# Hybrid decoder step: the second recurrence's sample outputs taken from the old states, its state update moved behind the output projection

## The reference, cut to what matters

```
S_t = diag(f_t) S_{t-1} + k_t v_t^T        o_t = S_t^T q_t
```

## Time and profile before

| | |
|---|---|
| median of three runs | 1176.42 us (1174.89 to 1178.26) |
| the profiled execution | 1168.96 us |
| its span, first to last instruction | 1167.1 us |
| TensorE matmuls busy | 1078.2 us (92%), 8206 |
| VectorE, ScalarE, GpSimd busy | 658.5, 395.5, 95.5 us |
| mean granted TensorE clock | 0.944 |

### The profile page before, as it was taken

The page is one execution under the profiler, slowest core; times in us unless marked ns, Lnnn a source line. Parts: engine busy times, 40 slices in busy tenths (PEclk is TensorE's granted clock), DMA queues, the critical chain, the costliest instruction groups (busy, mean ns, idle before and its releaser), DMA issues.

```text
span 1167.1 us, 20544 instructions
## 1 busy us (share of the span) xinstructions
PE 1078.2 (92%) x8206; PEld 911.1 (78%) x8206; DVE 658.5 (56%) x1422; ACT 395.5 (34%) x741; POOL 95.5 (8%) x194
## 2 busy tenths in 40 slices
PE   7998999879997999999999988888999789999997
PEld 5878878757873899999998633545888569999997
DVE  6865471334204588987646465565231447999742
ACT  3523221503134444444411313312213454444430
POOL 0010021210000012221000000000000001222100
PEclk9997889958998899999999988889999899999999
DMA  8330125313445555555443676557444465555540
GB/s 320 140 108 8 39 77 181 108 44 107 145 164 204 190 180 181 182 208 195 172 176 133 240 238 224 172 172 271 175 132 176 149 248 187 181 181 192 208 149 38
DMA packets 41569, 192.40 MB, mean 165 GB/s; under 512 B 4603, under 2 KB 5755, under 8 KB 24579
## 3 DMA queue, kind: packets, MB, share of 16 engines
q1 hardware_dynamic: 37298, 175.76, 43.1%
q0 software_dynamic: 3136, 13.76, 3.2%
q10 hardware_dynamic: 1040, 1.57, 0.4%
HBM read 183.72 MB, written 7.35 MB: 164 GB/s over the span
## 4 chain that ended last, share of the span: by engine, by line
PE 73%; issue 9%; DVE 7%; ACT 3%; DMA 3%; SPq 3%; POOL 1%; DVEq 0%; ACTq 0%; POOLq 0%
PE bank L1193 72%; DVE work L1790 2%; PE bank L1196 1%; SPq L625 1%; ACT work L776 1%; DVE work L1793 1%; SPq L611 1%; DMA ring<-in_cv 1%; DMA ring<-in_gu 1%; ACT work_r L776 1%; DVE smx L1874 0%; DVE ring_r L1790 0%; DMA ring<-in_pool_v 0%; DMA x<-in_x 0%; ACT hr L776 0%
## 5 line engine op out<-in xcount | busy, mean ns | idle before, releaser
L1193 PE MATMUL bank<-h,ring 128*128 128x264 f32 x896 | 207.3, 389 | 0.0
L1193 PE MATMUL bank<-h_r,work_r 128*128 128x264 f32 x704 | 200.6, 285 | 0.2 <-DVE sq_r L1793 0.2
L1193 PE MATMUL bank<-h_r,ring_r 128*128 128x264 f32 x704 | 200.2, 284 | 0.0
L1193 PE MATMUL bank<-sq_r,work_r 128*128 128x264 f32 x704 | 199.8, 284 | 0.0
L1193 PEld LDWEIGHTS bank<-h,ring 128*128 128x128 f32 x896 | 170.6, 191 | 31.3 <-issue 2.3
L776 ACT ACTIVATE work_r<-ring 128x2048 fp32r<-128x2048 f32 (+1 forms) x60 | 125.2, 2087 | 202.8 <-PE bank L1193 191.1
L1790 DVE TENSOR_TENSOR ring_r<-ring,work_r 128x2048 fp32r<-128x2048 f32 (+1 forms) x60 | 150.3, 2506 | 47.0 <-ACT work_r L776 47.0
L1193 PE MATMUL bank<-work 64*64 64x64 f32 (+13 forms) x1424 | 118.9, 279 | 24.0 <-ACT work L776 7.4
L1193 PE MATMUL bank<-work_r 128*128 128x264 f32 x704 | 129.7, 285 | 3.3 <-DVE ring_r L1790 3.1
L1193 PEld LDWEIGHTS bank<-h_r,work_r 128*128 128x128 f32 x704 | 132.3, 188 | 0.6 <-DVE sq_r L1793 0.4
L1193 PEld LDWEIGHTS bank<-sq_r,work_r 128*128 128x128 f32 x704 | 132.5, 188 | 0.1
(11 more groups left out here) (251 smaller groups left out, 1165.1 us busy)
## 6 DMA issues: line engine op xcount, KB each, us to landing
ring<-in_gu SPq DMA_DIRECT2D x44, 1024.0 KB, 4.9
ring<-in_down SPq DMA_DIRECT2D x16, 1408.0 KB, 6.0
ring<-in_pool_k SPq DMA_DIRECT2D x64, 256.0 KB, 3.3
ring<-in_pool_v SPq DMA_DIRECT2D x64, 256.0 KB, 3.2
ring<-in_ev_in_a SPq DMA_DIRECT2D x8, 1024.0 KB, 6.8
ring<-in_ev_in_b SPq DMA_DIRECT2D x8, 1024.0 KB, 4.8
ring<-in_ck SPq DMA_DIRECT2D x8, 1024.0 KB, 4.7
ring<-in_cv SPq DMA_DIRECT2D x8, 1024.0 KB, 5.9
```

Source lines behind the costliest of these rows:

```text
L1193: return nc.tensor.matmul(out, lhsT, rhs, start=start, stop=stop, skip_group_check=True)
```

## The change

The sample outputs of the second recurrence are computed from the old states, right behind the input projection and ahead of the transposes: VectorE forms qfs = q f and qks = q k on the samples' 32 columns, TensorE runs 128 matmuls of one column on shs and one of 32 columns with the block-diagonal ones (the sum k . q on all rows of a head), VectorE multiplies by zi and adds into oT. GpSimd's load of the memory rows and its decay of shs wait for that group. `state_update` goes behind the eight tiles of `ev_out` on TensorE and behind `residual_summed` on VectorE; the store of the new states follows it. The first four tiles of `ev_out` are computed in halves: chunks 0 to 3 between and after the heads' sums, chunks 4 to 7 afterwards. In layer 1 the first halves of tiles 0 and 1 of `od_out` go ahead of the wait for the gated unit. mh and mk change places in work. The diff, cut (left out: semaphore names, ScalarE's lines that lose `so_copy`, asserts):

```diff
@@ -210,6 +210,7 @@
     lin("ev_in_b", 16, 2, 2048, 12, lambda m: order.append(("hn", "gdn", m - 12)))
+    order.append(("sO", "hgrn"))
     for t in range(NCH):
@@ -218,14 +219,13 @@
         order.append(("ho", g))
-    for i in range(HC):
-        order.append(("su", "hgrn", i))
-    order.append(("sO", "hgrn"))
     for c in range(HC):
     lin("ev_out", KC, 2, 2048, 4)
+    for i in range(HC):
+        order.append(("su", "hgrn", i))
     memory(0)
@@ -489,6 +489,8 @@
         d2, e = place(e, HC, L)
+        qfs, e = place(e, HC, NS)
+        qks, e = place(e, HC, NS)
         assert e <= WORK - HC * T, e
@@ -500,8 +502,8 @@
-        mh, e = place(0, KC, NM)
-        mk, e = place(e, MH, NM)
+        mh, _ = place(XX + 2048, KC, NM)
+        mk, e = place(2048, MH, NM)
         mv, e = place(e, MH, NM)
@@ -685,7 +687,8 @@
-            pool.wait_ge(shs_in, 16)
+            full(pool, ("sO", "hgrn"))
+            pool.dma_start(h[:, :, 0:NM], A["memx"]).then_inc(memx_in, 16)
             nc.gpsimd.tensor_tensor(shs, shs, zf[:, :, L:T].unsqueeze(3).broadcast_to([128, HC, NS, HD]),
@@ -695,13 +698,15 @@
             store(A["o_hgrn"], SH[0], hg_stored)
-            pool.wait_ge(sst_ready, 8)
-            store(A["o_shs"], shs, hg_stored)
-                full(pool, ("lin", "ev_in_b", 15) if l == 0 else ("sx", "moba"))
-                pool.dma_start(h[:, :, 0:NM], A["memx"]).then_inc(memx_in, 16)
+                if l == 0:
+                    pool.wait_ge(sst_ready, 8)
+                    store(A["o_shs"], shs, hg_stored)
+                else:
+                    full(pool, ("sx", "moba"))
+                    pool.dma_start(h[:, :, 0:NM], A["memx"]).then_inc(memx_in, 16)
                 pool.wait_ge(hn_done, hn_no[(f"memk{l}", MH - 1)] + 1)
@@ -1000,13 +1005,12 @@
                 o_copy(("ho", (t, p)), p, 0, t)
-            so_copy("hgrn")
+            for g in G4:
+                drained(act, ("ho", g))
             headnorm("hgrn", HC, T, 1.0 / HD, out_rows("hgrn"))
                 act.wait_ge(memx_in, 16 * (l + 1))
-
-                act.wait_ge(hg_stored if l == 0 else kv_stored, 32)
                 for m in range(KC):
@@ -1014,6 +1018,8 @@
             def memory(l):
+                if l:
+                    act.wait_ge(kv_stored, 32)
                 for m in range(MH):
@@ -1049,6 +1055,8 @@
                 samples_out(name, mos, MH)
+                if l == 0:
+                    act.wait_ge(hg_stored, 32)
                 weights_high(l, 0)
@@ -1243,6 +1251,19 @@
                 end(ins)
+
+            def half_product(name, m, k0, src, ready=None):
+
+                b = open_(("lin", name, m)) if k0 == 0 else bank(("lin", name, m))
+                s = slot_of[(name, m)]
+                pe.wait_ge(ring_full[s % SLOTS], slot_value[s])
+                for k in range(k0, k0 + 4):
+                    if ready and m == 0:
+                        ready(k)
+                    o = ((m % 2) * KC + k) * 128
+                    ins = mm(b[:, 0:T], ring[:, s % SLOTS, o:o + 128], src[:, k, 0:T], k == 0, k == KC - 1)
+                if k0:
+                    close(ins, ("lin", name, m))
@@ -1475,6 +1496,15 @@
                     hn("gdn", m - 12, T, bd)
+            pe.wait_ge(hq_ready, 1)
+            pe.wait_ge(shs_in, 16)
+            b = begin(("sO", "hgrn"))
+            for c in range(HC):
+                for s in range(NS):
+                    for p in range(2):
+                        ps = slice(64 * p, 64 * p + 64)
+                        mm(b[ps, c * NS + s:c * NS + s + 1], shs[ps, c, s, :], qfs[ps, c, s:s + 1])
+            end(mm(b[:, 32:64], bd, qks.rearrange("p c s -> p (c s)")))
             pe.wait_ge(hg_dve, 2)
@@ -1521,14 +1551,19 @@
                                     close(ins, ("ho", (t, p)))
-            state_update("hgrn", hws2, 3)
-            state_out("hgrn", shs, zq, 2)
+            pe.wait_ge(mix_ready, 4)
+            half_product("ev_out", 0, 0, mix)
             for c in range(HC):
                 hn("hgrn", c, T, bd)
-            for m in range(KC):
-                if m == 4:
-                    norm(norms.index(("memkv", 0)))
-                lin("ev_out", m, KC, 2, mix, T, lambda k: pe.wait_ge(mix_ready, k + 1))
+                if c % 2:
+                    half_product("ev_out", 1 + c // 2, 0, mix)
+            half_product("ev_out", 3, 0, mix)
+            for m in range(4):
+                half_product("ev_out", m, 4, mix, lambda k: pe.wait_ge(mix_ready, k + 1))
+            norm(norms.index(("memkv", 0)))
+            for m in range(4, KC):
+                lin("ev_out", m, KC, 2, mix, T)
+            state_update("hgrn", hws2, 3)
@@ -1769,10 +1804,14 @@
                 drained(pe, ("O", "moba", j))
+            drained(pe, ("sx", "moba"))
+            for m in range(2):
+                half_product("od_out", m, 0, mix)
             for c in range(HC):
                 drained(pe, ("lin", "glu", 2 * c))
-            drained(pe, ("sx", "moba"))
-            for m in range(KC):
+            for m in range(2):
+                half_product("od_out", m, 4, mix)
+            for m in range(2, KC):
                 if m == 4:
@@ -2153,9 +2192,17 @@
             tt(kx, kx, zk[:, :, 0:L], ALU.mult).then_inc(hg_dve, 1)
+            tt(qfs, zq[:, :, L:T], zf[:, :, L:T], ALU.mult)
+            tt(qks, zq[:, :, L:T], zk[:, :, L:T], ALU.mult).then_inc(hq_ready, 1)
             dve.wait_ge(zg_ready, 4)
                      gated(zg, 0))
+            drained(dve, ("lin", "ev_in_b", 11))
+            full(dve, ("sO", "hgrn"))
+            b = bank(("sO", "hgrn"))
+            ob, pb = [b[:, 32 * i:32 * i + 32].rearrange("p (c s) -> p c s", c=HC) for i in range(2)]
+            step(tt(qks, zi[:, :, L:T], pb, ALU.mult))
+            drain(tt(oT[:, :, L:T], qks, ob, ALU.add), ("sO", "hgrn"))
             dve.wait_ge(att_zero, 1)
@@ -2175,7 +2222,6 @@
                     drain(V.tensor_copy(nxt, kv), key)
-            state_update("hgrn", hws1, shs, zk, 2)
             headnorm("hgrn", HC, T, lambda i: oT[:, i, :], lambda i: col("hgrn_norm"), lambda i: tmp[:, i % 2, :],
@@ -2192,6 +2238,7 @@
             residual_summed("ev_out", 0)
+            state_update("hgrn", hws1, shs, zk, 2)
```

More of the change, by code:

```diff
@@ L400, in build @@
         w_ready, sdec_ready, sst_ready = sem("w_ready"), sem("sdec_ready"), sem("sst_ready")
-        fk_ready, lf_ready, dec_ready, exp_ready, hg_dve, hg_pool, att_zero = [
-            sem(n) for n in ("fk_ready", "lf_ready", "dec_ready", "exp_ready", "hg_dve", "hg_pool", "att_zero")]
+        fk_ready, lf_ready, dec_ready, exp_ready, hg_dve, hg_pool, att_zero, hq_ready = [
+            sem(n) for n in ("fk_ready", "lf_ready", "dec_ready", "exp_ready", "hg_dve", "hg_pool", "att_zero", "hq_ready")]
         smax_ready, p_exp, p_ready = [sem(n) for n in ("smax_ready", "p_exp", "p_ready")]
```

## The result

The changed kernel takes 1162.52 us (median of four runs, 1156.71 to 1163.77), the kernel before 1175.66 beside it (four runs, 1171.91 to 1178.26). The ratio is 0.9881, 95% interval 0.9838 to 0.9924: 13.1 us faster, three fifths of what I forecast (21.8), and 1.5 us above the upper end of my range. The profiled execution took 1162.72 us, span 1160.8. Further down, a whole time is followed by its ratio to the kernel before, timed beside it, and the ratio's 95% interval.

What follows compares the result with a forecast made beforehand. It took the samples' state update, hand-overs between two long TensorE streams, as the bound. Gains of 23.6 behind `ho` and 1.4 in layer 1, less 2.0 and 1.2 ahead, made 21.8: 1154.6 us from 1176.42, range 1148.5 to 1161.

Steps and rivals of the forecast that it cites:

- layer 1: Before `od_out`: two half tiles (1.8 us) cover TensorE's wait of 1.43, 1.4 gained, ends 0 and 1.6.
- D: Rival, half tiles: TensorE stands still at one for a bank or slot until mix; gain 18.6, 1157.8 us; chance 0.08.
- E: Rival, slower: TensorE stays at 1.2 GHz through `ev_out`; 1192.6 us; chance 0.03.
- The sign: Whole kernel: faster 0.94, same 0.03, slower 0.03.
- a half tile 0.9, a tile 3.6: Projection behind `ho`: one matmul costs 0.226 us; four half tiles and four sums counted as 8 us.
- my landmarks: Stretch behind `ho`, rebuilt in us after its end, up to the memory projection at +32.6 instead of 56.2.
- My bound for being wrong: Behind `ho`: the forecast is wrong if the stretch to the memory projection exceeds 38 us; 28 to 34 expected.
- rival C: Ahead of `ho`: GpSimd's decay blocks VectorE's state chain, 3.3 us more; gain 18.5, 1157.9 us; chance 0.05.
- My order in time: Ahead of `ho`: decay at about 228 to 231.6, VectorE's first product of two SBUF operands at about 232.7; price 0.
- The clock ahead: Ahead of `ho`: clock may fall in the one-column products or transposes; 1.2 us lost taken, ends 0 and 3.8.
- rival A: Ahead of `ho`: clock falls before the transposes, the full 3.8 instead of 1.2; gain 19.2, 1157.2 us; chance 0.22.
- rival B: In `ho`: the clock lasts through it, up to 5.9 us gained; gain up to 27.7, 1148.7 us; chance 0.06.

Runs made afterwards that it cites:

- e2: Changed kernel with GpSimd's load of the memory rows moved behind the first prompt outputs, its decay left right behind the sample outputs: 1161.47 us (0.9900).
- e3: Changed kernel with the first four tiles of `ev_out` computed whole, behind the heads' sums: 1165.59 us (0.9934).
- e4: Changed kernel with the second recurrence's state update back between `ho` and the heads' sums, sample outputs still early: 1167.42 us (0.9960).
- the third execution: The changed kernel unedited, a third time (e11): 1162.7 us (0.9914).
- e1: Changed kernel with GpSimd's decay alone moved behind the first prompt outputs, its load of the memory rows left: 1163.55 us (0.9894).
- e5: Changed kernel with GpSimd's load of the memory rows and its decay both behind the first prompt outputs: 1164.9 us (0.9928).
- e6: e5 plus the memory norm's sum after five tiles instead of four, in both layers: 1158.21 us (0.9850).
- e10: e6 repeated unedited: 1159.34 us (0.9891).
- e11: The changed kernel unedited, run beside e10: 1162.7 us (0.9914).
- e8: e6 with the sample outputs between `kv` and `ho` instead of ahead of the transposes: 1160.46 us (0.9881).

## Why the prediction was partly wrong

- **Most of the mechanism held.** The products fit ahead of the transposes, no wait for GpSimd is left, half tiles run under the roots, `su` takes 3.60, layer 1 gains 1.5 (forecast 1.4). No transfer and no bank held TensorE, so D and E fell. The sign was right.
- **The step that failed: "a half tile 0.9, a tile 3.6", worked out as "one matmul of the projection costs 0.226".** The row behind it has 64 records in 14.48 us. For the half tile I took a record for a matmul. One fp32 matmul of a projection leaves two records: `half_product` issues four, and the trace shows 8, 0.45 us a matmul at 2.4 GHz; the 64 were four tiles. So the four early halves and the sums did not take 8 us with TensorE waiting for mix behind them. They took 11.8 (254.18 to 262.39, and two halves more at 1.8), longer than the roots, and TensorE, never idle, was what ended last. Against my landmarks, in us after `ho`: VectorE's first gain +7.4 (forecast +5.6), tile 0 closed +13.7 (+9.4), tile 3 +19.1 (+12.1), the sum +20.5 (+14.4), the memory projection +38.7 (+32.6). From the sum on it is 18.2 either way, so all of the miss of 6.1 lies ahead of the sum. VectorE's timeline of the changed kernel has the landmarks (first gain, last mix, residuals of tile 0 and tile 3):

```profile
261.57 0.49 DVE L1832 SCALAR_TENSOR_TENSOR tmp<-oT,vec,hr 128x264 f32<-128x264 f32 x1 [14.70 <-ACT hr L781]
...
265.19 0.43 DVE L1829 TENSOR_TENSOR mix<-tmp,work 128x264 f32<-128x264 f32 x1
267.93 0.43 DVE L1829 TENSOR_TENSOR x<-x,bank 128x264 f32<-128x264 f32 x1 [2.31 <-PE bank L1201]
...
273.34 0.43 DVE L1829 TENSOR_TENSOR x<-x,bank 128x264 f32<-128x264 f32 x1 [0.56 <-PE bank L1201]
```

VectorE has the last chunk of mix at 265.6 and waits 2.31 for TensorE, the other way round than I forecast. The prediction held both readings side by side: a tile of 3.6, and 14.75 for four, is right, and the half tile of 0.9 beside it is a quarter of a tile. The three halves of tiles 1 to 3 behind mix were priced at 0.9 too, so VectorE's adds of 1.3 per tile looked like the slower side there and the wait before the sum came out at 2.3; it was 1.47. My bound for being wrong, a stretch over 38 us, was passed.
- **GpSimd's decay (rival C, taken at 0): a block happened,** though of the last gate product and not of the state chain, in two of three executions of the changed kernel, and in e2 and e3; not in e4. The Trainium skill (SBUF — State Buffer, "Who interferes with whom") says that a VectorE operation with two SBUF inputs and a GpSimd operation that reads SBUF exclude each other, the later one being held for the whole of the first, and e2's 3.80 beside a multiply of 3.62 agrees; the product that began 0.76 ahead of the multiply and was held all the same does not fit by its records. My order in time was what failed. I let VectorE leave its gains at 227.97 and the decay start at about 228, and called them apart, while the last product of that very chain is an operation of two SBUF operands. The block cost less than its 4.3 on VectorE: 1.2 on the way to the end of `ho` against the third execution (26.9 against 25.7), 2.2 against e1 (24.7), where `ho` also began at the high clock.
- **The clock ahead (1.2 taken, up to 3.8 in rival A).** It fell ahead of the transposes or in them in every variant with the products ahead of them: 2.51 to 3.25 for sixteen instead of 1.91. So A's event is the rule. Its price was 0.7 in the changed kernel, and 1.3 in the third execution. It was not 3.8, since the clock was soon back (0.96 from 235.6 to 239.2). In the changed kernel it slowed the first half of `att` too (2.08 for 16 records, 2.06 for all 32 before), but behind that TensorE had to wait for VectorE's held product anyway. My 1.2 was of a fair size. Forecast ahead: 3.2 lost. Measured: 5.0 = products 4.1, less the two waits 2.0, transposes 0.7, and 2.2 for the block and the clock in `kv` and `ho`.
- **The clock of `ho` (rival B):** 0.50 throughout in the changed kernel, as taken. Where the decay was moved (e1, e5, e6, e10) the first 1.5 us of `ho` ran at 1.00 and it took 11 us instead of 12.

In one sum: 17.5 behind `ho` instead of 23.6, less 5.0 instead of 3.2 ahead, and 1.5 in layer 1: 14.0 instead of 21.8. From 1168.96 that gives 1155.0 for the profiled execution, which took 1162.72; the 7.7 between them are untouched parts of the span: 4.5 longer ahead of the stretch, 3.7 longer behind `od_out`, and 0.4 shorter between the memory projection and glu. Such differences show between executions of one kernel too (the table).

**What stays open.** Why the product at 232.03 is held although the multiply's record starts 0.76 later, when e1 shows that the load's issue, which stood between, holds nothing. What brings the clock down ahead of `ho`. The transposes are not needed for it: in e2, e4 and e11 it fell inside the one-column products, before the first transpose (0.82 or 0.83 in their last microsecond), in e8 inside them too, and in the first recurrence no transposes are near. That the products are the cause is not shown. And what decides, from one execution to the next, where the clock falls in untouched parts.

## What to carry to other kernels

Before you price a part of an operation by its records, check how many records the whole has in the code and price the whole again by your figure; here a float32 matmul is two. When an elementwise operation of GpSimd gets a new release, look at what VectorE has on its queue within about a microsecond of it (held at 0.76 ahead, free at 1.11), and put the release where VectorE waits for something. And where executions differ by more than the edit is worth, compare the edit's own stretch in several traces and give the whole time beside it.

## What the runs showed of the hardware

- A VectorE product of 0.43 us with two SBUF operands took 4.69 and 3.80 beside a GpSimd multiply of 3.6, and 0.43 beside the issue of a GpSimd DMA of 0.96.
- In each trace with the 128 one-column records (3.90 us, TensorE busy throughout) ahead of the transposes, the clock fell in them or within 2 us behind them. In the untouched first recurrence it fell in or behind the like products in eleven of thirteen traces (after: 80 records in 21.01 us, 0.50), and not in those of before and e4 (18.07).
- A float32 matmul of 128x264 leaves two records, 0.45 us at 2.4 GHz (8 records in 1.81) and 0.97 at 1.2 GHz (8 in 3.89).
- Three executions of the changed kernel differed by 4 us ahead of the stretch (223.0 to 227.3) and by 6 between the memory projection and `od_out` (533.1 to 539.1). Over the twelve traces of the changed kernel and its variants, whose TensorE work in both parts is the same, it was 8 (221.6 to 229.5) and 11 (532.7 to 543.4).
